# First norm on three engines with partial sums on TensorE, and the halo stages reordered

## The reference

```
h = rmsnorm(x, g_mix);  q, k, v, u, qm = split(h @ w_in)
y_attn = dilated sliding windows (128,1), (512,4), (2048,16), ALiBi, merged by softmax denominators
y_pool = (trailing means over 2, 4, 8, 16 tokens - u) @ w_pool * pool_scale
y_mem  = softmax(qm @ km^T / 8) @ vm,   km, vm from rmsnorm(mem, g_mem) @ w_mem_kv
x = x + concat(y_attn, y_pool, y_mem) @ w_out
x = x + relu(rmsnorm(x, g_ffn) @ w_ff1)^2 @ w_ff2
out = rmsnorm(x, g_final)
```

## Time and profile before

| what | us |
|---|---|
| time, median of 3 runs (range) | 1625.96 (1623.55 to 1628.05) |
| the profiled execution | 1639.09 |
| its span, slowest core (core 3) | 1638.0 |
| spans of the eight cores | 1605.7 to 1638.0 |
| PE busy on core 3 | 1558.9 (95%) |
| DVE, ACT, POOL busy on core 3 | 944.4, 722.9, 161.1 |

### The profile page before, as it was taken

The page is one execution under the profiler, slowest core; times in us unless marked ns, Lnnn a source line. Parts: engine busy times, 40 slices in busy tenths (PEclk is TensorE's granted clock), DMA queues, the critical chain, the costliest instruction groups (busy, mean ns, idle before and its releaser), DMA issues.

```text
span 1638.0 us, 27926 instructions; the slowest of 8 cores (1605.7 to 1638.0 us)
## 1 busy us (share of the span) xinstructions
PE 1558.9 (95%) x9722; PEld 755.0 (46%) x9722; DVE 944.4 (58%) x1378; ACT 722.9 (44%) x1085; POOL 161.1 (10%) x219
## 2 busy tenths in 40 slices
PE   4989899989899999999999999999999999999996
PEld 1434534544355444544445544544455544544442
DVE  4665555556366555666465565666475565545654
ACT  3645554442445436453354436353354435354222
POOL 3121110010101001000100010000100000000001
PEclk9998788999999999999999999999999999999998
DMA  9767446686978668574765665343833463343542
GB/s 243 178 213 230 116 68 133 110 177 201 219 162 191 182 215 229 149 202 164 234 191 138 217 208 191 129 155 130 295 116 143 155 228 121 128 172 138 186 151 101
DMA packets 43241, 282.93 MB, mean 173 GB/s; under 512 B 5344, under 2 KB 7520, under 8 KB 10976
## 3 DMA queue, kind: packets, MB, share of 16 engines
q0 software_dynamic: 17952, 121.45, 31.0%
q1 hardware_dynamic: 24576, 158.64, 27.7%
q10 hardware_dynamic: 576, 1.05, 0.2%
HBM read 286.69 MB, written 46.92 MB: 204 GB/s over the span
## 4 chain that ended last, share of the span: by engine, by line
PE 85%; DMA 5%; DVE 4%; ACT 3%; issue 3%; POOL 1%; ACTq 0%; DVEq 0%; SPq 0%; POOLq 0%
PE mm L350 73%; PE ob L652 6%; PE sc L629 4%; DMA X<-xh 2%; DMA ring<-wall 2%; PE sc L350 2%; DVE val L663 1%; ACT P L631 1%; ACT rt L768 1%; DVE acc L381 1%; ACT Vd L355 0%; DMA cpc_t<-cpc 0%; DVE aT L775 0%; POOL Vd L268 0%; DVE P L636 0%
## 5 line engine op out<-in xcount | busy, mean ns | idle before, releaser
L350 PE MATMUL mm<-h2T,ring 128*128 128x512 bf16 x2192 | 517.6, 386 | 15.2 <-ACT rt L768 12.7
L350 PE MATMUL mm<-aT,ring 128*128 128x512 bf16 x2048 | 472.0, 382 | 5.4 <-DMA ring<-wall 3.8
L631 ACT ACTIVATE P<-sc 128x1024 bf16<-128x1024 f32 x256 | 247.5, 1023 | 209.2 <-PE sc L629 208.4
L350 PEld LDWEIGHTS mm<-h2T,ring 128*128 128x128 bf16 x2192 | 206.5, 99 | 265.5 <-issue 60.5
L775 DVE TENSOR_TENSOR aT<-rt 128x512 bf16<-128x512 f32 x232 | 184.1, 793 | 214.5 <-ACT rt L768 212.3
L350 PEld LDWEIGHTS mm<-aT,ring 128*128 128x128 bf16 x2048 | 193.4, 98 | 220.7 <-issue 15.5
L768 ACT ACTIVATE rt<-mm 128x512 f32<-128x512 f32 x232 | 138.3, 596 | 240.2 <-PE mm L350 185.9
L636 DVE TENSOR_TENSOR P<-P,E 128x1024 bf16<-128x1024 bf16 x224 | 154.2, 694 | 135.1 <-ACT P L631 134.1
L371 ACT ACTIVATE sq<-X 128x512 f32<-128x512 f32 x196 | 121.8, 627 | 182.6 <-DVE X L801 109.8
L652 PE MATMUL ob<-P,Vd 128*128 128x128 bf16 x1792 | 140.9, 223 | 12.3 <-DVE val L663 11.0
L652 PEld LDWEIGHTS ob<-P,Vd 128*128 128x128 bf16 x1792 | 119.6, 100 | 70.4 <-issue 30.6
(11 more groups left out here) (108 smaller groups left out, 939.3 us busy)
## 6 DMA issues: line engine op xcount, KB each, us to landing
ring<-wscratch SPq DMA_DIRECT2D x123, 1024.0 KB, 5.9
ring<-wall POOLq DMA_DIRECT2D x48, 1024.0 KB, 9.8
X<-xh POOLq DMA_DIRECT2D x22, 1024.0 KB, 16.4
wscratch<-ring SPq DMA_DIRECT2D x21, 1024.0 KB, 4.7
X<-xr POOLq DMA_DIRECT2D x16, 1024.0 KB, 10.4
out<-X POOLq DMA_DIRECT2D x14, 1024.0 KB, 9.4
vscratch<-Vd POOLq DMA_DIRECT2D x24, 192.0 KB, 7.1
Vd<-vscratch POOLq DMA_DIRECT2D x6, 768.0 KB, 9.8
```

The costliest lines, as they stand in the source:

```text
L350: T.op("pe", lambda: nc.tensor.matmul(out_ap, lhsT=l, rhs=r, start=(i == 0), stop=(i == n - 1)), reads=rd, writes=[b_out], mark=(i == n - 1))
L631: T.op("act", lambda: nc.scalar.activation(out=P_[:], in_=s_[:], func=AF.Exp, scale=0.125), reads=[bs_], writes=[bP_])
```

## The change

Seven edits, all of them in the first 135 us:

1. A one-column Square on ACT right after `ones` is set, ahead of everything else on ACT.
2. The weights of V, K and u/qm are loaded in halves (chunks 0 to 3, chunks 4 to 7), each with a semaphore; for tile 0 the matmuls of a half wait for that half alone. Later users wait for the second half's.
3. K's weights and x of tile 2 are issued ahead of the flag copies on POOL.
4. The first norm (`stat_first`) has no chain of adds: ACT squares chunks 0 to 3, 4, 5 and 7, DVE chunk 6; DVE adds three pairs, and five float32 matmuls against `ones` sum chunk 0, chunk 1, 2+3, 4+6 and 5+7 in one PSUM bank.
5. K of tile 0 is made chunk by chunk (`ksweep`) into four banks, mm0, mm1, ob0, ob1; the statistics of tile 1 come between its second and third quarter and use a bank of sc.
6. In the halo tiles, V of blocks 0 and 1 is copied out by DVE and blocks 2 and 3 by ACT; blocks 0 to 2 are issued before the first K group and block 3 after the statistics.
7. Tile 5's norm, made beside tile 4: squares from group 8 instead of 6, `stat` before group 15 instead of 11, norms from 15.5.

The first rows of PE: before, one statistics matmul stands ahead of the V sweep, and the next tile's inside K.

```diff
+        T.op("act", lambda: nc.scalar.activation(out=den[:, 0:1], in_=ones[:, 0:1], func=AF.Square),
+             reads=[b_ones], writes=b_den)
...
         def load_w(pi):
-            T.dma("pool", cast_sem[SLOT[pi]], ring[SLOT[pi]][:], wall[pi], writes=[b_ring[SLOT[pi]]])
+            s_ = SLOT[pi]
+            T.dma("pool", half_sem[pi], ring[s_][:, 0:2048], wall[pi][:, 0:2048], writes=[b_half[pi]])
+            T.dma("pool", cast_sem[s_], ring[s_][:, 2048:4096], wall[pi][:, 2048:4096], writes=[b_ring[s_]])
...
         load_x("pool", xbuf(1), xh[1])
+        load_w(P_K)
+        load_x("pool", xbuf(2), xh[2])
         for s_ in range(NHALO - 1):
...
-        load_w(P_K)
-        load_x("pool", xbuf(2), xh[2])
...
+            def stat_first(self):
+                S = [(s_[:], b_) for s_, b_ in SQ_EARLY] + [
+                    (Pbuf[i][:].rearrange("p h t -> p (h t)").bitcast(F32), b_P[i]) for i in (2, 3)]
+                m_, bm_ = next_mm()
...
+                for k in range(4):
+                    sq_("act", k, k)
+                add((self.acc, self.b_acc), S[2], S[3])
+                part(0, S[0][0], [S[0][1]])
+                part(1, S[1][0], [S[1][1]])
+                part(2, self.acc, self.b_acc)
+                sq_("act", 4, 4)
+                sq_("dve", 6, 2)
+                sq_("act", 5, 5)
+                add(S[4], S[4], S[2])
+                sq_("act", 7, 3)
+                part(3, S[4][0], [S[4][1]])
+                add(S[5], S[5], S[3])
+                part(4, S[5][0], [S[5][1]])
+                self.rstd(m_, bm_)
...
+                    if j == 0:
+                        bp = [b_half[P_V]] if q < 2 else [b_ring[SLOT[P_V]]]
...
+            def ksweep(q):
+                def f():
+                    pk = ring[SLOT[P_K]][:].rearrange("p (k c) -> p k c", k=8)
+                    bp = [b_half[P_K]] if q < 2 else [b_ring[SLOT[P_K]]]
+                    outs = [(mm[0][:], b_mm[0]), (mm[1][:], b_mm[1]), (ob[0][:], b_ob[0]), (ob[1][:], b_ob[1])]
+                    sweep([[(pk[:, k, ol * 128:(ol + 1) * 128], h3[:, k, :], bp + [bh[k]]) for k in range(8)]
+                           for ol in range(4)], outs, q)
+                    if q == 3:
+                        for ol in range(4):
+                            fevac(P_K, ol, *outs[ol])
+                return f
...
-                evac("dve" if j == NHALO + 1 else "act", d4[:, :, 0::2, :],
+                evac("dve" if j == NHALO + 1 or (j < NHALO and b < 2) else "act", d4[:, :, 0::2, :],
...
-        ln = stage_A(0)
-        for _, f in ln_side(ln, 0, 1, 8, 9, 1):
-            f()
         lns = [stage_A(j) for j in range(NHALO + 2)]
+        lns[0].stat_first()
+        for k in range(8):
+            lns[0].norm(k)
...
-                side = squares(ln, 2.9, 0.01) + [(5, ln.stat)] + norms(ln, 5.1, 0.3)
+                side = squares(ln, 0.9, 0.01, 0, 4) + squares(ln, 2.9, 0.01, 4, 8)
+                side += [(5.9, lambda ln=ln: ln.stat(SC_EARLY[0]))] + norms(ln, 5.91, 0.3)
...
-            run(groups, side + [(4.01, v_out)])
+            run(groups, side + [(4.0, lambda: v_out(0, 3)), (4.9, lambda: v_out(3, 4))])
...
-            side += ln_side(lns[j + 1], 6, 0.5, 11, 11.5, 0.5)
+            side += ln_side(lns[j + 1], 8, 0.5, 15, 15.5, 0.5)
```

More of the change, by code:

```diff
@@ L258, in build_nc @@
         SLOT = {P_V: 0, P_UM: 1, P_K: 2}
+        b_half = {pi: Buf(f"half{pi}") for pi in SLOT}
+        half_sem = {pi: dsem(f"halfsem{pi}") for pi in SLOT}
         def load_w(pi):
-            T.dma("pool", cast_sem[SLOT[pi]], ring[SLOT[pi]][:], wall[pi], writes=[b_ring[SLOT[pi]]])
+            s_ = SLOT[pi]
+            T.dma("pool", half_sem[pi], ring[s_][:, 0:2048], wall[pi][:, 0:2048], writes=[b_half[pi]])
+            T.dma("pool", cast_sem[s_], ring[s_][:, 2048:4096], wall[pi][:, 2048:4096], writes=[b_ring[s_]])
         load_x("pool", xbuf(0), xh[0])
@@ L382, in square, with stat, rstd @@
                      reads=[bs_], writes=self.b_acc)
-            def stat(self):
-                m_, bm_ = next_mm()
+            def stat(self, bank=None):
+                m_, bm_ = bank or next_mm()
                 mm_ops(m_[:, 0:self.n], bm_, [(ones[:], self.acc, [b_ones] + self.b_acc)])
+                self.rstd(m_, bm_)
+            def rstd(self, m_, bm_):
                 T.op("act", lambda: nc.scalar.activation(out=self.acc, in_=m_[:, 0:self.n], func=AF.Ln, bias=EPS),
@@ L390, in stat, with sq_, add, part @@
                      reads=self.b_acc, writes=self.b_acc)
+            def stat_first(self):
+                S = [(s_[:], b_) for s_, b_ in SQ_EARLY] + [
+                    (Pbuf[i][:].rearrange("p h t -> p (h t)").bitcast(F32), b_P[i]) for i in (2, 3)]
+                m_, bm_ = next_mm()
+                def sq_(e, k, i):
+                    s_, bs_ = S[i]
+                    if e == "act":
+                        T.op("act", lambda: nc.scalar.activation(out=s_, in_=self.x3[:, k, :], func=AF.Square),
+                             reads=[self.b_x[k]], writes=[bs_])
+                    else:
+                        T.op("dve", lambda: nc.vector.tensor_tensor(out=s_, in0=self.x3[:, k, :], in1=self.x3[:, k, :],
+                                                                    op=ALU.mult), reads=[self.b_x[k]], writes=[bs_])
+                def add(o, a, b):
+                    T.op("dve", lambda: nc.vector.tensor_tensor(out=o[0], in0=a[0], in1=b[0], op=ALU.add),
+                         reads=[a[1], b[1]], writes=o[1] if isinstance(o[1], list) else [o[1]])
+                def part(i, r, rd):
+                    T.op("pe", lambda: nc.tensor.matmul(m_[:], lhsT=ones[:], rhs=r, start=(i == 0), stop=(i == 4)),
+                         reads=[b_ones] + rd, writes=[bm_])
+                for k in range(4):
[12 more added lines that the diff above has]
+                part(4, S[5][0], [S[5][1]])
+                self.rstd(m_, bm_)
             def gain(self, k, in_place=False):
@@ L461, in f, with vsweep_out @@
                     pk, bp = st["v"]
+                    if j == 0:
+                        bp = [b_half[P_V]] if q < 2 else [b_ring[SLOT[P_V]]]
                     sweep([[(h_tok(b, k), pk[:, k, :], bp + [bh[k]]) for k in range(8)] for b in range(4)], SC_EARLY, q)
                 return f
-            def vsweep_out():
-                for b in range(4):
+            def vsweep_out(lo, hi):
+                for b in range(lo, hi):
                     vevac(b, b == 3, *SC_EARLY[b])
+            def ksweep(q):
[9 more added lines that the diff above has]
+                return f
             def usweep(q):
@@ L561, in stage_B @@
                 groups = [usweep(q) for q in range(4)] + groups
-            groups += [fgroup("k", P_K, ol, ol == 3) for ol in range(4)]
+            groups += [ksweep(q) for q in range(4)] if j == 0 else [fgroup("k", P_K, ol, ol == 3) for ol in range(4)]
             if own:
@@ L912, in build_nc @@
                 load_w(P_UM)
-                side = squares(ln, 2.9, 0.01) + [(5, ln.stat)] + norms(ln, 5.1, 0.3)
+                side = squares(ln, 0.9, 0.01, 0, 4) + squares(ln, 2.9, 0.01, 4, 8)
+                side += [(5.9, lambda ln=ln: ln.stat(SC_EARLY[0]))] + norms(ln, 5.91, 0.3)
             if j == 1:
                 load_x("pool", xbuf(4), xh[4])
-                side = squares(ln, 0, 0.4) + [(5, ln.stat)] + norms(ln, 5.1, 0.25) + squares(lns[3], 7.3, 0.2, 0, 4)
+                side = squares(ln, 0, 0.4) + [(4.2, ln.stat)] + norms(ln, 4.3, 0.3) + squares(lns[3], 7.3, 0.2, 0, 4)
             if j >= 2:
```

## The result

The changed kernel takes 1616.24 us in the median of its four runs, the kernel before 1625.7 in the same comparison: a ratio of 0.9938, with an interval from 0.9917 to 0.9958. The saving is 9.5 us by the medians and 10.1 by the ratio, where the prediction said 12.4 (1613.5).

A forecast was written before the change was run, and what follows sets the result against it. PE, busy for 95% of the span, was taken to bound the kernel. Terms of 4.4, 2.5 and 5.5 us sum to 12.4, taking the median from 1625.96 to 1613.5 us, with a range of 1607 to 1623.

The forecast's parts named there:

- Term 1: From the start to tile 1's V sweep: a gain of 4.4 us, bounds 1.1 and 5.8.
- V's end before 29.2 buys nothing: Tile 0: K's first half lands at about 29.2 us, so ending the V sweep sooner gains nothing.
- early issue puts K into the same place of the queue: Start: K's weights stand in a full DMA queue behind tile 1's x, so issuing them sooner does not move them.
- Term 2: Tiles 1 to 3: waits of 1.12 twice and 0.57 go, 2.8 us; net 2.5, bounds 1.5 and 2.8.
- 0.3 ahead of the statistics: Tile 1: DVE's norms lead by some 2 us instead of 2.8; adds end about 0.3 us after the statistics' turn.
- Term 3: Tile 4: the wait before tile 5's statistics and the clock dip go; net 5.5 us, bounds 3.5 and 6.5.
- The 4.01: Tile 4: PE's wait of 4.01 us before tile 5's statistics, claimed to go, with the slower clock after it.
- a margin of 0.5: Tile 4: DVE's adds end at 118.5 us, PE reaches the statistics' new place at 119.1, half a microsecond to spare.
- the 0.3 that I gave back: Tile 4: PE's memory groups wait a little for DVE's copies of the memory tokens' K and V; 0.3 us.
- The poor start: Rival: the start gains only 1.1 us, so 9.1 in all, or 1616.9 us; chance 0.13.
- eaten by the loads of x: Rival: PE waits longer for x near 430 us on core 5, up to all 12.4; 1626 us, chance 0.10.
- The lower clock: Rival: a low-clock stretch falls on one core of each timed run, adding 24.0 us; 1637.5 us, chance 0.07.

The follow-up runs named there:

- e6: The changed kernel without the early one-column Square on ACT; V sweep of tile 1 starts at 36.64 us, one total of 1725.49 us.
- e7: The changed kernel with POOL's flag copies again ahead of the issue of K's weights and tile 2's x; V sweep of tile 1 starts at 36.78 us.
- e5: The changed kernel with K's weights of the start in one 2 MB DMA again; V sweep of tile 1 starts at 42.42 us.
- e2_late_stat: The kernel before with edit 7 alone (tile 5's squares, statistics and norms later); 1617.56 us, ratio 0.9927.
- e1_blockbufs: The changed kernel with one tracked buffer for each of the four V blocks instead of one for all; 1611.82 us, ratio 0.9894.
- e3: The changed kernel without edits 6 and 7, so edits 1 to 5 on the start alone; 1619.5 us, ratio 0.9962.
- e4: The kernel before with edit 6 alone (DVE copies V of blocks 0 and 1, block 3 copied behind the statistics); 1635.46 us in one run.
- e9: The changed kernel with ACT's copy of V block 2 issued behind the statistics with block 3's; tile 1 15.26 us, tile 2 14.79 us.
- e8: The changed kernel with the old chain of squares and adds for the first norm, early Square kept; V sweep of tile 1 starts at 38.57 us.

## Why the prediction came close, and where it failed

**Term 1, the start: 4.4 predicted, 4.0 measured** (V1 from 41.23 to 37.24). Its steps held: five matmuls from 10.69 on core 0, the last two at full clock (2.01 us together) and done at 17.95 (18.2 predicted), a wait for K's first half that ends at 28.87 in the mean (29.2 predicted), none for the second, V1 in the middle of 36 to 38. V ran at full clock on six cores; on cores 1 and 4 the clock fell to 0.5 inside the sweep, which the wait for K hid. "V's end before 29.2 buys nothing" is e6; that early issue puts K into the same place of the queue is e7; the halves are e5. What the sum left out is the clock after K's wait: three of the eight cores, core 3 among them, ran the first K quarters at half speed.

The page "DMA: Bandwidth & Descriptors" of the Trainium skill (section "Anatomy of one DMA — SWDGE (gpsimd) path") gives some 2.0 us of fixed cost per DMA; as an estimate from it, K's first half would have come at about 31, with one DMA more ahead of it than before, V's second half (the prediction counts two, but one makes the 31). Measured, as the mean of the eight cores, the first half landed at 28.63. The second half, with two DMAs more in the queue than before, landed at 31.84, where all of K landed at 31.93 before the change and at 32.17 in e5: the traces show no such cost between DMAs that stand in a full queue.

**Term 2, tiles 1 to 3: 2.5 predicted, 0.6 measured. This is the step that failed.** It said that "Ln starts as soon as the statistics are out, and the third K group finds its bank read 1 us ahead". The old waits did go: tile 3, whose V goes into a buffer for each block, is 0.73 shorter. And the third group did find its bank read. But in tiles 1 and 2 the second group, which had not waited before, found its bank unread, and Ln itself came 1.2 us after the statistics in tile 1. I counted DVE's two copies as load on DVE (1.5 us in a tile of 16) and as ready for the statistics' bank, and did not follow who waits for them: ACT's copy of block 2, by the tracked buffer that all four blocks share, and behind it in ACT's order K's first copy. The shorter lead of DVE, for which I had put 0.3 ahead of the statistics (0.35 measured), also moved this whole chain by 1.5 us in tile 1: the waits of 1.46 and 0.57 had no term in the sum. With a buffer for each block, tiles 1 to 3 are 2.68 us shorter than before (51.13 to 48.45), where 2.5 stood. So the term was right for a kernel without that link.

**Term 3, tile 4: 5.5 predicted, 6.3 measured**, 5.6 on the four cores of before that had lost the least of their clock there (33.50 to 27.88). The 4.01 and the half-clock time after it went. The adds were 0.87 us early where a margin of 0.5 was predicted. The memory groups wait 0.37 and 0.23 on core 0, as they did before (0.38 and 0.23 on core 3), so the 0.3 that I gave back for them was not needed.

**The sum.** 4.0 + 0.6 + 6.3 = 10.9; V of tile 5 starts 10.6 us earlier (0.3 goes in tile 4's u groups, 7.65 us long where they were 7.34), and 9.5 to 10.1 arrive in the total. That this is near the 12.4 is in part luck: term 2 fell short by 1.9 and term 3 exceeded its size by 0.8. In the profiles, on the six cores whose clock wasn't at 0.81 before, the gain is 10.6 at 180 us and 9.5 at 200: what went is a fall of the clock at 180, behind a wait for POOL that is as long in both kernels (2.07 and 2.08). Before, none of these six cores lost the clock there; after, cores 0 to 5 did, and three cores of e2_late_stat and two of e1_blockbufs did too. Whether this makes the difference in the timed runs isn't shown. The stretch 180 to 184 us after the change, on core 0 and on core 7:

```profile
180.00:184.00 4.00, 4.00 (x12) 1.51 (x11) 0.95 (x2) 0.63 (x1) 0.00 (x0) 0.57 0.96 252
```

```profile
180.00:184.00 4.00, 3.89 (x19) 1.79 (x20) 1.38 (x2) 1.26 (x2) 0.00 (x0) 1.00 0.96 250
```

The parts alone (e2, e3, e4) start V of tile 5 by 5.8, 4.4 and 3.2 us earlier, 13.4 together. The change has 10.6, e1_blockbufs 13.1: the missing 2.8 are nearly all the link between ACT and DVE. The totals stand in the same order if, of the runs timed beside e1, e2 and e3, only those are taken in which every core's mean clock was above 0.98 (a limit set afterwards): their means are 1621.9 us for the kernel before (12 runs), 1618.2 for e3 (7), 1616.9 for e2 (9), 1614.3 for the changed kernel (6) and 1610.1 for e1_blockbufs (4). By these the change gains 7.7, and the buffers 4.1 more.

**The rivals.** The poor start did not come (4.0, not 1.1). Nothing was eaten by the loads of x: on core 5 the wait of the earlier trace rows comes 13.3 us earlier and is not longer:

```profile
414.65 3.40 PE L359 MATMUL mm<-h2T,ring 128*128 128x512 bf16 x8 [5.54 <-ACT rt L833]
```

The lower clock did not spread: no core of the changed kernel's profile is below 0.989, and none in the runs that its two ratios count is below 0.988.

## What to carry to other kernels

When work moves to a second engine, ask for each moved instruction not only what it reads but what it shares a tracked buffer with, and what stands behind the one that then waits; e9 shows that a change of order is as good a cure as more buffers. A shorter lead of one engine over another is a cost by itself: measure the length of its chain against the start of the stage that waits for it. Behind a full queue earlier issue buys nothing (e7), and faster work in front only as much as it would otherwise end behind the landing (nothing in e6, 1.3 us in e8); splitting the transfer so that its first half can be used does.

## What the runs showed of the hardware

An idle time of the same length may or may not be followed by the lower clock level. The wait of 1.46 in tile 1, which follows a wait of 0.35 (0.49 in e8) and one statistics matmul, lowered the clock on none of eight cores in the first profile of the changed kernel, on one in the second, and on four in e8; the wait of 2.07 to 2.08 near 180 us on six of eight cores after the change, and on none of the six undisturbed cores before. What decides it was not settled by these runs.

The level of 0.81 took two cores of a die in both profiles that hold it: cores 4 and 5 of e4 for 157 us (0.975 and 0.973 in the mean, cores 6 and 7 at 0.990 and 0.993), as cores 2 and 3 did before. The page "TensorE: Matmul & The Clock Gate", Part 1, of the Trainium skill tells of 13/16 of the clock for a whole die once three of its cores run dense matmuls; in these two profiles the level agrees, the whole die doesn't. Both profiles with it have the old wait in tile 4, and none with edit 7 shows it; e3, which has the wait, doesn't show it in its profile either. In the timed runs, two or more cores of a die are at a mean of 0.970 to 0.975 in 10 of the 23 of the kernel before that stand beside e1, e2 and e3, and in 3 of 11 of e3 (all four cores in three of these 13), but also in one of six of e1_blockbufs (0.975 and 0.974), which has edit 7. So no cause is claimed.
